# Norms around the first expert stage: sums made with the residual, norm and modulation applied chunk by chunk

## The chip, the cores and the metric

The kernel runs on one NeuronCore of a Trainium2 chip, in float32. The metric is the device time of one execution in microseconds (us). TensorE (PE) multiplies matrices into PSUM, VectorE (DVE) and ScalarE (ACT) work on tiles of 128 partitions, GpSimd (POOL) here mostly issues gathers by index, and SyncE (SP) issues the transfers of weights. The engines run their own instruction lists and meet at semaphores.

## The reference, cut to what matters

The model is two stacks one after the other on 512 tokens of width 1024. What the change touches is the second layer of the first stack from its pooling mixer on, and the start of the second stack:

```
x = layer_norm(DN_ALPHA * x + gt1 * y, ln_g[1, 0], ln_b[1, 0])          # y: the pooling mixer's output
x = layer_norm(DN_ALPHA * x + gt2 * moe_swiglu(x * (1 + sc2) + sh2),    # 8 experts, each token goes to 2
               ln_g[1, 1], ln_b[1, 1])
# second stack
u = _rmsnorm(x, norm1_w)
proj = u @ w_in                                                         # the in-projection
```

`layer_norm` takes mean and variance over the 1024 features of a token, `_rmsnorm` the mean square; x is needed after both, as the residual.

## The kernel before

The residual `k.x` lies with features on the partitions: 8 chunks (KC) of 128 features by 512 tokens. So a mean over features is a sum over partitions, and TensorE makes it: a 128x128 square of ones times each chunk, accumulated over the 8 chunks in one PSUM bank (`k.ps` has 8 banks), which leaves the sum in every partition. A float32 matmul of 128x512 shows as two MATMUL records in the trace, a transpose as one.

The program is a row of stages; nearly each stands in an `nc.Block()` of its own. At a block's end all engines meet before any goes on. Order within a block is the order of the code, engine by engine; there is no scheduler. The stages that matter:

- `stage_pool` (line 1762): modulates x, pools it on VectorE, multiplies by `pl_w` on TensorE, and adds the gated product to x chunk by chunk (L1819).
- `stage_layer_norm(k, 1, 0)` (line 1490): TensorE sums the 8 chunks (L1505); VectorE divides by D (L1517) and subtracts the mean from each chunk (L1520); ScalarE squares (L1533), TensorE sums the squares (L1509), ScalarE takes the root (L1535), VectorE its reciprocal (L1522) and the products (L1525), ScalarE applies g and b (L1539).
- `stage_modulate(k, h, 1, 3)` (line 1547): VectorE makes `h = x * (1 + sc2) + sh2` in 8 instructions (L1553).
- `route(k, r, h)` (line 1932): TensorE multiplies h by the router's weights (L2001, 32 matmuls of 32x128), transposes h into rows (L2008) that ScalarE copies and stores, VectorE picks the experts, ranks them by their counts, and makes the lists of tokens. Once the experts are ranked, SP starts on the first expert's weights.
- the expert block (from line 2772): POOL gathers the rows of the first expert, TensorE transposes them (L2818) and multiplies (L2881 up, L2888 down). VectorE first copies the transposed rows (L3153) and then multiplies x by DN_ALPHA (L2291, `joined.scale_x`). An expert takes 152 tokens at most here; what is beyond goes through a loop at the end. Then `Combine` joins: for each of 4 tiles of 128 tokens POOL gathers the two rows of each token (L2284), VectorE weights and adds them (L2312, L2314), TensorE transposes the sum (L2326), and VectorE adds it to x, gated, chunk by chunk (L2305).
- `stage_layer_norm(k, 1, 1)`, and `stage_rms_norm(k, u, norm1)` (line 3217): ScalarE squares x (L3229), TensorE sums (L3238), root (L3231), reciprocal (L3244), and u is made (L3247). SP issues the first three pieces of `w_in` in this block (L3269).
- the in-projection's block (line 3277): TensorE multiplies u by 6 pieces of `w_in` (L3295), ScalarE copies out.

## Time and profile before

| | us |
|---|---|
| median of 3 runs (lowest, highest) | 3457.12 (3450.19, 3457.69) |
| the profiled execution, its own time | 3453.89 |
| span of the profiled execution | 3452.0 |
| TensorE busy | 2894.8 (84%) |
| VectorE busy | 1115.6 (32%) |
| ScalarE busy | 538.2 (16%) |
| mean granted TensorE clock | 0.911 of full speed |

Times in the trace count from the span's start. The share of busy time is a mean over stages with different limits, so what counts in the rows further down is which engine's instruction ends last before the next stage can start. The granted clock is 1.00 at 2.4 GHz and 0.50 at 1.2 GHz.

### The profile page before, as it was taken

The numbers are of one execution on the slowest core, as the hardware profiler recorded it, in microseconds if no ns is written. First come the engines' busy times: TensorE is split into PE (matmuls) and PEld (weight loads), VectorE is DVE, ScalarE is ACT, GpSimd is POOL, SyncE is SP. The second block draws the span as 40 slices with busy tenths as digits, with TensorE's granted clock in tenths as the row PEclk, the third lists the DMA queues.
The fourth block names the chain that finished last, engine by engine and source line by source line (L and its number), as shares of the span: only waits on it lengthen the run. The fifth ranks groups of instructions, "written<-read, shape, count | busy, mean of one in ns | idle before, by whom it ended". The sixth has DMA issues, their size and how long they took to land. (4 is left out here: it accounts for less than half of the span.)

```text
span 3452.0 us, 58296 instructions
## 1 busy us (share of the span) xinstructions
PE 2894.8 (84%) x25919; PEld 1887.8 (55%) x25919; DVE 1115.6 (32%) x1781; ACT 538.2 (16%) x964; POOL 210.2 (6%) x200
## 2 busy tenths in 40 slices
PE   7998488898887799999579999994897876877784
PEld 2545388888623344445268889882343634544442
DVE  4323578787452001143621111103105623110112
ACT  0001233333121000001100000102003601000001
POOL 0110121111010000000010000000000001000000
PEclk8997699999978899998779999997998987999997
DMA  8622222111221822560099999512301008999994
GB/s 313 196 99 84 82 69 65 48 39 51 73 95 49 204 73 73 178 241 32 28 269 356 345 344 326 216 68 69 117 24 68 1 0 322 427 426 427 427 427 175
DMA packets 241556, 597.92 MB, mean 173 GB/s; under 512 B 24540, under 2 KB 131582, under 8 KB 225816
## 3 DMA queue, kind: packets, MB, share of 16 engines
q1 hardware_dynamic: 210008, 488.85, 38.6%
q0 software_dynamic: 17664, 51.97, 5.3%
q10 hardware_dynamic: 13632, 53.32, 4.0%
q8 instruction: 209, 3.42, 0.4%
q14 instruction: 43, 0.35, 0.0%
HBM read 547.25 MB, written 46.83 MB: 172 GB/s over the span
## 5 line engine op out<-in xcount | busy, mean ns | idle before, releaser
L1658 PE MATMUL ps<-ffn_h,ffn_wb 128*128 128x512 f32 x704 | 306.6, 598 | 33.4 <-DMA ffn_wb<-in_ffn_w 17.9
L2881 PE MATMUL ps<-moe_xt,moe_wb 128*128 128x152 f32 (+2 forms) x2112 | 303.4, 306 | 3.8 <-DMA moe_wb<-in_moe_w 2.1
L2482 PE MATMUL ps<-hier_wb,hier_xt 128*64 128x256 f32 x2048 | 245.1, 396 | 73.1 <-DMA hier_wb<-in_expert_w_up 34.9
L2881 PEld LDWEIGHTS ps<-moe_xt,moe_wb 128*128 128x128 f32 x2112 | 291.5, 192 | 17.0 <-issue 3.9
L2482 PEld LDWEIGHTS ps<-hier_wb,hier_xt 128*64 128x64 f32 x2048 | 162.2, 142 | 167.4 <-issue 70.9
L1658 PEld LDWEIGHTS ps<-ffn_h,ffn_wb 128*128 128x128 f32 x704 | 135.2, 192 | 204.9 <-issue 204.9
L868 PE MATMUL ps<-AT,X 64*64 64x64 f32 x4608 | 164.3, 229 | 34.2 <-DVE X L1160 29.8
L868 PEld LDWEIGHTS ps<-AT,X 64*64 64x64 f32 x4608 | 154.9, 144 | 46.8 <-DVE X L1160 34.6
L1726 PE MATMUL ps<-ffn_g,ffn_wd 128*128 128x512 f32 x352 | 153.0, 598 | 3.0 <-PEq L1617 3.0
L2498 PE MATMUL ps<-hier_wb,hier_actT 128*64 128x512 f32 x512 | 120.3, 613 | 17.9 <-DMA hier_wb<-in_expert_w_down 12.2
L3295 PE MATMUL ps<-in_u,in_wb 128*128 128x512 f32 x256 | 113.1, 604 | 10.0 <-PEq L3222 10.0
L1726 PEld LDWEIGHTS ps<-ffn_g,ffn_wd 128*128 128x128 f32 x352 | 67.4, 192 | 88.6 <-issue 88.6
L2888 PE MATMUL ps<-moe_hT,moe_wb 128*128 128x152 f32 (+1 forms) x880 | 112.8, 290 | 0.0
L2888 PEld LDWEIGHTS ps<-moe_hT,moe_wb 128*128 128x128 f32 x880 | 111.2, 190 | 0.2
L1686 DVE SCALAR_TENSOR_TENSOR ffn_th<-ffn_th,ps 128x512 f32<-128x512 f32 x22 | 15.1, 687 | 293.4 <-ACT ffn_th L1671 293.4
L3161 DVE SCALAR_TENSOR_TENSOR moe_th<-moe_th,ps 128x152 f32<-128x152 f32 (+2 forms) x75 | 25.1, 335 | 249.9 <-ACT moe_th L3039 249.9
L2620 DVE COPY hier_xt<-ps 128x1024 f32<-128x1024 f32 x16 | 19.6, 1225 | 224.9 <-PE ps L2474 224.9
L3295 PEld LDWEIGHTS ps<-in_u,in_wb 128*128 128x128 f32 x256 | 49.6, 194 | 73.3 <-issue 73.3
L1169 DVE TENSOR_TENSOR AT<-AT,ps 128x512 f32<-128x512 f32 x120 | 79.0, 684 | 28.4 <-PE ps L868 26.2
L2498 PEld LDWEIGHTS ps<-hier_wb,hier_actT 128*64 128x64 f32 x512 | 36.4, 139 | 79.0 <-issue 62.8
L1533 ACT ACTIVATE ln_sq<-x 128x512 f32<-128x512 f32 x32 | 19.4, 630 | 381.4 <-DVE x L1520 381.4
L1152 DVE STREAM_TRANSPOSE Y<-AT 128x512 f32<-128x512 f32 x120 | 77.8, 686 | 0.0
(527 smaller groups left out, 4089.7 us busy)
## 6 DMA issues: line engine op xcount, KB each, us to landing
moe_wb<-in_moe_w SPq DMA_DIRECT2D x54, 2048.0 KB, 12.3
hier_wb<-in_expert_w_gate SPq DMA_DIRECT2D x32, 2048.0 KB, 37.8
hier_wb<-in_expert_w_up SPq DMA_DIRECT2D x32, 2048.0 KB, 38.0
hier_wb<-in_expert_w_down SPq DMA_DIRECT2D x32, 2048.0 KB, 38.4
moe_wb<-in_moe_w SPq DMA_DIRECT2D x27, 1536.0 KB, 10.1
ada_late<-in_ada_w ACTq DMA_DIRECT2D x8, 3072.0 KB, 10.2
ffn_wb<-in_ffn_w SPq DMA_DIRECT2D x22, 1024.0 KB, 7.8
ada_rest<-in_ada_w POOLq DMA_DIRECT2D x64, 256.0 KB, 3.3
```

Source lines behind the costliest of these rows:

```text
L868: mm = pe.matmul(k.ps[rows_of(c), g, q * C:(q + 1) * C], X[rows_of(c), at, :], AT[rows_of(c), at, :], start=True, stop=True)
L1152: dve.transpose(group(Y, g), group(AT, g)).then_inc(flipped, 1)
L1169: dve.tensor_tensor(m, m, bank8(g), ALU.add).then_inc(updated, 1)
L1658: mm = pe.matmul(k.ps[:, bank + q, :], wb[:, j, q, c, o * P:(o + 1) * P], h[:, c, :], start=c == 0, stop=c == KC - 1)
L1726: mm = pe.matmul(k.ps[:, j, :], wd[:, j, c, :], g[:, c, :], start=c == 0, stop=c == FC - 1)
L2482: mm = pe.matmul(k.ps[both_halves(a), bank, 0:256], xs[:, c, :], wb[:, slot, at:at + 256], start=c == 0, stop=c == KC - 1)
L2498: mm = pe.matmul(k.ps[both_halves(a), 7, :], at_sb[:, c, :], wb[:, slot, at:at + 512], start=c == 0, stop=c == 3)
L2620: dve.tensor_copy(xt[:, q % 2, :, :].rearrange("p (a c) n -> p a (c n)", a=2), k.ps[:, 4:6, :]).then_inc(xt_ready, 1)
L2881: mm = pe.matmul(k.ps[:, bank, 0:width], wb[:, slot, at:at + P], xs[:, c, 0:width], start=c == 0, stop=c == KC - 1)
L2888: mm = pe.matmul(out_columns(o)[:, 0:width], wb[:, slot, at:at + P], hT[:, f, 0:width], start=f == 0 and o % 3 == 0, stop=f == FC - 1 and ...
L3161: dve.scalar_tensor_tensor(th[:, slot, 0:width], th[:, slot, 0:width], 1.0, k.ps[:, gate, 0:width], ALU.add, ALU.mult)
L3295: mm = pe.matmul(k.ps[:, e % 6, :], own[:, piece] if kind == "fm" else tokens[:, piece], tokens if kind == "fm" else own, start=c == 0, st ...
```

## The change

Four things change.

The pooling stage and `Combine` make the sum over features themselves. In the pooling stage VectorE adds the chunks of x up in a tile of its own after each chunk (`ChunkSums.add`), and TensorE sums that tile over the partitions in one matmul. In `Combine.turn` TensorE runs, for each tile of tokens, 8 matmuls of ones by the finished 128 columns of x into bank 4, one tile behind the transposes.

The block of `stage_layer_norm(k, 1, 0)` and that of `stage_modulate` go. `route` takes a `Norm`: VectorE subtracts the mean straight from PSUM, ScalarE squares, TensorE sums the squares, VectorE multiplies by the reciprocal root, and ScalarE makes h from the scaled x in one instruction per chunk, with g, b, scale and shift folded into two small vectors (`factors`). The router's matmuls wait for h chunk by chunk.

x itself with g and b, times DN_ALPHA, is made by ScalarE at the start of the expert block (`norm.residual`); `joined.scale_x` goes, and `Combine.add` waits for it.

The block of `stage_layer_norm(k, 1, 1)` and that of `stage_rms_norm` go too; both norms run at the head of the in-projection's block, where SP issues the first pieces of `w_in`. ScalarE squares g * x + b in one instruction into u, TensorE sums each chunk as it comes, VectorE meanwhile writes x, and the first in-projection matmul waits for u chunk by chunk.

```diff
@@ stage_pool, vector @@
                     dve.scalar_tensor_tensor(k.x[:, o, :], k.ps[:, o, :], gate[:, o:o + 1], k.x[:, o, :],
                                              ALU.mult, ALU.add)
+                    sums.add(dve, o)
@@ stage_pool, tensor @@
+                sums.total(pe)
@@ new @@
+class Norm:
...
+    def centre(self, dve):
+        k = self.k
+        for c in range(KC):
+            dve.scalar_tensor_tensor(k.x[:, c, :], k.ps[:, self.sums_in, :], -1.0 / D, k.x[:, c, :], ALU.mult, ALU.add).then_inc(
+                k.centred.sem, 1)
+
+    def factors(self, dve, scale=None, shift=None):
+        dve.tensor_scalar(self.own[:, 0, :], self.g, self.alpha, None, ALU.mult)
+        dve.tensor_scalar(self.own[:, 1, :], self.b, self.alpha, None, ALU.mult)
+        if scale is not None:
+            dve.tensor_tensor(self.out[:, 0, :], self.g, scale, ALU.mult)
+            dve.tensor_tensor(self.out[:, 1, :], self.b, scale, ALU.mult)
+            dve.drain()
+            dve.tensor_tensor(self.out[:, 1, :], self.out[:, 1, :], shift, ALU.add)
+        dve.drain()
+
+    def squares(self, act):
+        k = self.k
+        act.activation(self.root[:, :], k.eps[:, 1:2], ACT.Sqrt)
+        for c in range(KC):
+            act.wait_ge(k.centred.sem, k.centred.at(c + 1))
+            act.activation(self.sqr[:, c, :], k.x[:, c, :], ACT.Square).then_inc(k.squared.sem, 1)
+        act.wait_ge(k.square_sums.sem, k.square_sums.at(1))
+        act.activation(self.rstd[:, :], k.ps[:, self.bank, :], ACT.Sqrt, scale=1.0 / D, bias=k.eps[:, 1:2])
+        act.drain().then_inc(k.rooted.sem, 1)
+
+    def sum_squares(self, pe):
+        for c in range(KC):
+            pe.wait_ge(k.squared.sem, k.squared.at(c + 1))
+            mm = pe.matmul(k.ps[:, self.bank, :], k.square("ones"), self.sqr[:, c, :], start=c == 0, stop=c == KC - 1)
...
+    def scale(self, dve, dst=None):
+        dve.wait_ge(k.rooted.sem, k.rooted.at(1))
+        dve.reciprocal(self.rstd[:, :], self.rstd[:, :])
+        dve.drain()
+        for c in range(KC):
+            dve.tensor_tensor(dst[:, c, :], k.x[:, c, :], self.rstd[:, :], ALU.mult).then_inc(k.scaled.sem, 1)
+
+    def modulated(self, act, h):
+        for c in range(KC):
+            act.wait_ge(k.scaled.sem, k.scaled.at(c + 1))
+            act.activation(h[:, c, :], k.x[:, c, :], ACT.Identity, scale=self.out[:, 0, c:c + 1],
+                           bias=self.out[:, 1, c:c + 1]).then_inc(k.h_made.sem, 1)
+
+    def residual(self, act):
+        for c in range(KC):
+            act.wait_ge(k.scaled.sem, k.scaled.at(c + 1))
+            act.activation(k.x[:, c, :], k.x[:, c, :], ACT.Identity, scale=self.own[:, 0, c:c + 1],
+                           bias=self.own[:, 1, c:c + 1]).then_inc(k.x_made.sem, 1)
...
+class ChunkSums:
...
+    def add(self, dve, o):
+        dve.drain()
+        if o == 1:
+            dve.tensor_tensor(self.sums[:, :], k.x[:, 0, :], k.x[:, 1, :], ALU.add)
+        elif o > 1:
+            dve.tensor_tensor(self.sums[:, :], self.sums[:, :], k.x[:, o, :], ALU.add)
+        if o == KC - 1:
+            dve.drain().then_inc(k.summed.sem, 1)
+
+    def total(self, pe):
+        pe.wait_ge(k.summed.sem, k.summed.at(1))
+        pe.matmul(k.ps[:, 0, :], k.square("ones"), self.sums[:, :], start=True, stop=True)
@@ route(k, r, h, norm=None), tensor @@
+                if norm:
+                    norm.sum_squares(pe)
...
+                        if norm and a == 0:
+                            pe.wait_ge(k.h_made.sem, k.h_made.at(c + 1))
@@ route, scalar @@
+                if norm:
+                    norm.squares(act)
+                    norm.modulated(act, h)
@@ route, vector, behind its small set-up instructions; on_vector is centre, factors and scale @@
+                if norm:
+                    norm.on_vector(dve, h)
@@ Combine.turn @@
+        def sums(q):
+            pe.wait_ge(k.free_v.sem, k.free_v.at(q + 1))
+            for c in range(KC):
+                pe.matmul(k.ps[:, sums_in, q * P:(q + 1) * P], k.square("ones"), k.x[:, c, q * P:(q + 1) * P],
+                          start=c == 0, stop=c == KC - 1)
...
             mm.then_inc(k.prod_v.sem, 1)
+            if q and sums_in is not None:
+                sums(q - 1)
+        if sums_in is not None:
+            sums(NT - 1)
@@ stage_first_moe @@
-                stage_layer_norm(k, 1, 0)
-                stage_modulate(k, h, 1, 3)
-                route(k, r, h)
+                norm = Norm(k, "10", k.v("ln_g10"), k.v("ln_b10"), s, alpha=DN_ALPHA, own=own_factors)
+                route(k, r, h, norm)
...
-                    joined.turn(pe)
+                    joined.turn(pe, 4)
...
+                    norm.residual(act)
...
-                    joined.scale_x(dve)
...
+                    dve.wait_ge(k.x_made.sem, k.x_made.at(KC))
                     joined.add(dve)
@@ build @@
-        stage_layer_norm(k, 1, 1)
@@ stage_in_projection @@
-        stage_rms_norm(k, u, k.v("norm1"), load_first)
+        norm = Norm(k, "11", k.v("ln_g11"), k.v("ln_b11"), s, sums_in=4)
@@ its block: sync @@
+                load_first(sp)
@@ tensor @@
+                norm.sum_squares(pe)
+                for c in range(KC):
+                    pe.wait_ge(k.x_made.sem, k.x_made.at(c + 1))
+                    mm = pe.matmul(k.ps[:, 7, :], k.square("ones"), u[:, c, :], start=c == 0, stop=c == KC - 1)
+                mm.then_inc(rms_sums, 1)
...
+                            if e == 0:
+                                pe.wait_ge(scaled_u, c + 1)
@@ scalar @@
+                norm.squares(act)
+                for c in range(KC):
+                    act.wait_ge(k.scaled.sem, k.scaled.at(c + 1))
+                    act.activation(u[:, c, :], norm.sqr[:, c, :], ACT.Square, scale=norm.own[:, 0, c:c + 1],
+                                   bias=norm.own[:, 1, c:c + 1]).then_inc(k.x_made.sem, 1)
+                act.wait_ge(rms_sums, 1)
+                act.activation(rms[:, :], k.ps[:, 7, :], ACT.Sqrt, scale=1.0 / D, bias=k.eps[:, 2:3])
+                act.drain().then_inc(rms_rooted, 1)
@@ vector @@
+                norm.centre(dve)
+                norm.factors(dve)
+                norm.scale(dve, norm.sqr)
+                dve.drain()
+                for c in range(KC):
+                    dve.tensor_scalar(k.x[:, c, :], norm.sqr[:, c, :], norm.own[:, 0, c:c + 1], norm.own[:, 1, c:c + 1],
+                                      ALU.mult, ALU.add)
                 dve.memset(lr[:, :], 1.0)
+                dve.wait_ge(rms_rooted, 1)
+                dve.reciprocal(rms[:, :], rms[:, :])
                 dve.drain()
+                for c in range(KC):
+                    dve.scalar_tensor_tensor(u[:, c, :], k.x[:, c, :], weight[:, c:c + 1], rms[:, :],
+                                             ALU.mult, ALU.mult).then_inc(scaled_u, 1)
```

## Rows read from the trace of the kernel before

**Rows 1.** Page, part 1: engine, busy us (share of the span), instructions.
```profile
PE 2894.8 (84%) x25919; PEld 1887.8 (55%) x25919; DVE 1115.6 (32%) x1781; ACT 538.2 (16%) x964; POOL 210.2 (6%) x200
```

**Rows 2.** Windows: length, busy us of each engine, granted clock, DMA share, GB/s.
```profile
1682.97:1718.76 35.79, 17.87 (x97) 9.19 (x97) 18.04 (x31) 11.28 (x17) 0.00 (x0) 0.81 0.00 1
1760.15:2357.65 597.50, 570.80 (x4208) 509.04 (x4208) 64.21 (x171) 50.33 (x123) 21.00 (x20) 0.98 0.76 269
2383.38:2433.31 49.93, 25.71 (x49) 10.62 (x49) 22.62 (x28) 17.51 (x27) 0.00 (x0) 0.74 0.36 129
```

**Rows 3.** Timeline, VectorE, pool to router: start, us, engine line op tiles xcount [idle before].
```profile
1675.84 4.70 DVE L1819 SCALAR_TENSOR_TENSOR x<-ps,pl_gate,x 128x512 f32<-128x512 f32 x7
...
1691.55 4.91 DVE L1520 TENSOR_TENSOR x<-x,ln_m 128x512 f32<-128x512 f32 x8 [0.44 <-issue]
...
1704.31 4.91 DVE L1525 TENSOR_TENSOR x<-x,ln_r 128x512 f32<-128x512 f32 x8
1711.08 3.74 DVE L1553 TENSOR_SCALAR moe_h<-x,mod 128x512 f32<-128x512 f32 x8 [1.87 <-PEq L1496]
...
1715.57 0.15 DVE L2079 TENSOR_SCALAR moe_iota_b<-iota 8x2 f32<-8x2 f32 x1
```

**Rows 4.** Timeline, TensorE, the same stretch.
```profile
1675.81 6.37 PE L1829 MATMUL ps<-pl_h,pl_w 128*128 128x512 f32 x8 [3.85 <-DVEq L1816]
1683.27 7.10 PE L1505 MATMUL ps<-x,sq 128*128 128x512 f32 x16 [1.09 <-PEq L1778]
1692.96 7.13 PE L1509 MATMUL ps<-ln_sq,sq 128*128 128x512 f32 x16 [2.58 <-ACT ln_sq L1533]
1715.12 3.64 PE L2001 MATMUL ps<-moe_h,moe_wr 128*32 128x128 f32 x64 [15.03 <-PEq L1549]
1718.70 1.11 PE L2008 MATMUL ps<-sq,moe_h 128*128 128x128 f32 x8
```

**Rows 5.** Timeline, ScalarE, the same stretch.
```profile
1705.04 5.75 ACT L1539 ACTIVATE x<-x,vec 128x512 f32<-128x512 f32 x8 [4.22 <-DVE x L1525]
```

**Rows 6.** Windows of 2 us: length, TensorE busy, granted clock, DMA share, GB/s.
```profile
1706.00:1708.00 2.00, 0.00 (x0) 0.50 0.00 0
...
2388.00:2390.00 2.00, 2.00 (x6) 1.00 0.00 0
```

**Rows 7.** Timeline, TensorE, start of the expert stage.
```profile
1760.15 40.08 PE L2881 MATMUL ps<-moe_xt,moe_wb 128*128 128x152 f32 x297 [0.57 <-DVE moe_xt L3153]
```

**Rows 8.** Timeline, VectorE, the same stretch.
```profile
1760.02 2.28 DVE L2291 TENSOR_SCALAR x<-x 128x4096 f32<-128x4096 f32 x1
```

**Rows 9.** Timeline, ScalarE, the same stretch.
```profile
1763.97 0.30 ACT L3039 ACTIVATE moe_th<-ps 128x152 f32<-128x152 f32 x1 [31.31 <-PE ps L2881]
```

**Rows 10.** Timeline, VectorE, joining to in-projection.
```profile
2379.15 4.23 DVE L2305 SCALAR_TENSOR_TENSOR x<-ps,mod,x 128x128 f32<-128x128 f32 x16
...
2393.64 4.90 DVE L1520 TENSOR_TENSOR x<-x,ln_m 128x512 f32<-128x512 f32 x8
...
2406.39 4.90 DVE L1525 TENSOR_TENSOR x<-x,ln_r 128x512 f32<-128x512 f32 x8
2424.02 3.35 DVE L3244 RECIPROCAL rms_r_in_u<-rms_r_in_u 128x512 f32<-128x512 f32 x1 [12.72 <-ACT rms_r_in_u L3231]
2427.45 5.39 DVE L3247 SCALAR_TENSOR_TENSOR in_u<-x,vec,rms_r_in_u 128x512 f32<-128x512 f32 x8
```

**Rows 11.** Timeline, TensorE, the same stretch.
```profile
2374.81 1.97 PE L2326 MATMUL ps<-sq,moe_yg 128*128 128x128 f32 x8 [7.30 <-DVEq L2315]
...
2383.70 9.13 PE L1505 MATMUL ps<-x,sq 128*128 128x512 f32 x16 [2.61 <-PEq L2771]
...
2413.82 9.44 PE L3238 MATMUL ps<-rms_sq_in_u,sq 128*128 128x512 f32 x16 [11.64 <-ACT rms_sq_in_u L3229]
2433.31 6.92 PE L3295 MATMUL ps<-in_u,in_wb 128*128 128x512 f32 x9 [10.05 <-PEq L3222]
```

**Rows 12.** Timeline, ScalarE, the same stretch.
```profile
2399.22 1.28 ACT L1535 ACT_TABLE_LOAD   x1
```

More of the change, by code:

```diff
@@ L198, in build @@
         k.stored = [sem(f"stored{n}") for n in range(2)]
+        k.summed, k.centred, k.squared = dma_sem("summed"), dma_sem("centred"), dma_sem("squared")
+        k.square_sums, k.rooted, k.scaled = dma_sem("square_sums"), dma_sem("rooted"), dma_sem("scaled")
+        k.h_made, k.x_made = dma_sem("h_made"), dma_sem("x_made")
         k.sq = sb("sq", [P, len(SQUARES), P])
@@ L1450, in stage_rwkv_out, with stage_project_residual @@
     k.p_for_v.base += KC
-def stage_project_residual(k, wb, z, gate, alpha=DN_ALPHA):
+def stage_project_residual(k, wb, z, gate, alpha=DN_ALPHA, sums=None):
     with k.nc.Block() as block:
@@ L1471, in _ @@
                 mm.then_inc(k.prod_v.sem, 1)
+            if sums:
+                sums.total(pe)
         @block.vector
@@ new lines, with __init__, close @@
+class ChunkSums:
+    def __init__(self, k, name, stack):
+        self.k, self.sums = k, k.sb(f"x_sums_{name}", [P, SEQ], stack=stack)
+    def add(self, dve, o):
+        k = self.k
+        dve.drain()
[6 more added lines that the diff above has]
+    def total(self, pe):
+        k = self.k
+        pe.wait_ge(k.summed.sem, k.summed.at(1))
+        pe.matmul(k.ps[:, 0, :], k.square("ones"), self.sums[:, :], start=True, stop=True)
+    def close(self):
+        self.k.summed.base += 1
@@ L1777, in stage_pool @@
         stage_modulate(k, h, 1, 0)
+        sums = ChunkSums(k, "pool", s)
         with nc.Block() as block:
@@ L1820, in _ @@
                                              ALU.mult, ALU.add)
+                    sums.add(dve, o)
             @block.tensor
@@ L1831, in _ @@
                         mm.then_inc(k.prod_v.sem, 1)
+                sums.total(pe)
     k.loaded[0].base += 16
@@ L1835, in stage_pool @@
     k.prod_v.base += KC
+    sums.close()
 ROUTER_LOADS = 9
@@ L1929, in overflow_pairs, with route @@
             engine.nop()
-def route(k, r, h):
+def route(k, r, h, norm=None):
     nc, t = k.nc, k.t
@@ L3209, in _ @@
                     overflow_pairs(dve, r, body)
+                    dve.wait_ge(k.x_made.sem, k.x_made.at(KC))
                     joined.add(dve)
             joined.close()
+            norm.close()
 def stage_rms_norm(k, dst, weight, sync=None):
@@ L3274, in load_first @@
             sp.dma_start(wl[:, :, :], src[:, :, att - 2 * GLA_RANK:att]).then_inc(k.loaded[0].sem, 16)
-        stage_rms_norm(k, u, k.v("norm1"), load_first)
+        norm = Norm(k, "11", k.v("ln_g11"), k.v("ln_b11"), s, sums_in=4)
+        rms = k.sb("in_rms", [P, SEQ], stack=s)
+        rms_sums, rms_rooted, scaled_u = (own_signal(k, s, f"in_{n}") for n in ("rms_sums", "rms_rooted", "scaled_u"))
+        weight = k.v("norm1")
         with nc.Block() as block:
@@ L3327, in stage_in_projection @@
     k.prod_v.base += 1
+    norm.close()
 def stage_mixers(k, qk, gg, gv, lr, q_, k_, v, mixed, wb, w):
```

34 lines of the change are left out of this document (32 added, 2 removed).

## The prediction, made before the changed kernel ran

> **What bounds the kernel now.** I read the page's table of engines first: TensorE is busy for 84% of the span [rows 1]. A gain off TensorE counts only where TensorE waits, so I next split the stretch around the change into windows [rows 2]. The expert stage, 597.50 us, is TensorE's: 570.80 busy at clock 0.98. Two stretches are not. From the last addition of the pooling stage to the end of the router's matmuls are 35.79 us, of which TensorE is busy for 17.87. From the last addition of the joining to the first in-projection matmul are 49.93 us, TensorE busy for 25.71, VectorE for 22.62. I call them A and B. In both each engine works while the others wait: one chain, so that each link taken out shortens the kernel until the next link is late. Last I read both stretches engine by engine in order of time; their links are the terms below.
>
> **Stretch A, start.** The seven additions to x start at 1675.84, 0.66 apart (4.70 less one of 0.75, by six), and an eighth ends at 1682.97, the window's start [rows 2, 3]. The change puts a drain behind each, and from the second on an addition. A drain costs 0.08 beyond its instruction (the reciprocal 2424.02 + 3.35, the next start 2427.45) [rows 10]; an addition of 128x512 keeps VectorE 0.60 (4.91 for 8) [rows 3]. So 0.83 for the first chunk and 0.83 + 0.60 for each other: 1675.84 + 0.83 + 7 x 1.43, and 0.16 for the last one's end and drain, is 1686.8, 3.9 later than now. No cover hides this: TensorE's products are done at 1682.18 [rows 4]. Then one matmul of ones, 0.89 at full clock (7.10 by 8) or 1.6 at half (6.37 by 4) [rows 4]; TensorE has stood 4.6 us by then, so I take 1.6: 1688.4. Now the sum ends at 1690.37.
>
> A block's change costs 0.30 (1682.97 to 1683.27), and route's small VectorE instructions, which stand ahead of the norm, end at 1715.72, 0.9 behind the modulation's end at 1714.82 [rows 3, 4]. So the subtraction starts at 1689.3, against 1691.55, since the mean's own instruction is gone as well: 2.2 won. From there to TensorE's first sum of squares are 1.41 now (1691.55 to 1692.96) [rows 3, 4], 1.5 with the sum read from PSUM: 1690.8.
>
> **The clock.** Now these 16 records take 7.13 because TensorE comes from the 7.10 us of the first sum and stands only 2.58 [rows 4]. After the change that work is gone, and what is ahead of the squares is one matmul in 8 us. Where TensorE starts on such work after little activity the same 16 records take 9.13 and 9.44 [rows 11]: half clock for the first 4 us or so, then 1.00 [rows 6]. I take 9.3: 1700.1, as late as now (1700.09). So all that the early sum won is given back by the clock. Beside that, the Trainium skill, "TensorE: Matmul & The Clock Gate", Part 1, says that the engine is at half rate by default and that activity releases it, so that taking work off TensorE can slow the rest. By that rule A's head comes out at nothing won, by the rows at full clock at 2.2; the trace agrees with it as far as 7.13 against 9.13 and 9.44 go.
>
> **Stretch A, end.** From the end of the squares' sum to the scaling 4.22 stay (1704.31 less 1700.09): 1704.3. ScalarE starts 0.73 behind it and takes 5.75 for 8 chunks [rows 3, 5]; now it writes x, then it writes h. The block change, the 3.74 of modulation and the wait of TensorE for all of it go. The router's matmuls, 3.64 by 8 = 0.46 a chunk, follow chunk by chunk: 1704.3 + 0.73 + 5.75 + 0.46 + 0.1 for the handover = 1711.4 in place of 1718.76. The factors, five small instructions of 0.15 to 0.2 with two drains, lie in VectorE's wait for the root (1696.5 to 1700.9). Won: 7.4.
> From this goes what TensorE then lacks in clock. Now the router's 3.64 us at half clock bring it up, and the transposes behind them run at 0.14 each (1.11 for 8) [rows 4]; spread over 5.75 us they may not, and a transpose at half clock takes 0.25 (1.97 for 8) [rows 11]. Eight to sixteen of those stand ahead of what VectorE waits for, at 0.11 each: 0.9 to 1.8. I take 1.0. A gives 6.4; its ends are 3.5 (all of route's short matmuls stay slow) and 9.5 (full clock in both places, 2.2 and 1.0 more).
>
> **The expert stage.** Its weights are requested and its first rows gathered when routing is done, so it moves as a whole. `residual` adds 8 instructions to ScalarE, 5.75 us [rows 5], at the block's start; ScalarE has stood 31.31 us when its first tanh comes [rows 9], which covers them. Without that cover the price would be the 5.75. `scale_x`, 2.28, ends at 1762.30, ahead of the tanh at 1763.97, while TensorE already multiplies [rows 7 to 9]: nothing won by its loss. The joining's new wait on x is met 600 us earlier.
>
> **Stretch B, the sums.** Each tile's 8 matmuls of 128x128 are 16 records. No row shows ones by 128 columns of x; the bounds are the transposes, 0.246 a record at half clock, so 3.9 a tile [rows 11], and the experts' 128x152 at full clock, 40.08 by 297 = 0.135, so 2.2 [rows 7]. Tile 0's lie in TensorE's idle 7.30 [rows 11]. Tile 1's come behind tile 2's transposes, from 2376.8 (2374.81 + 1.97) [rows 11], and at 3.9 end at 2380.7; the last transposes, now free to run when VectorE turns to tile 2's additions at 2379.15 [rows 10], stand behind them, 1.6 late, and end at 2382.7. VectorE's last 8 additions (half of 4.23) then end at 2384.9 and not at 2383.38. By then TensorE has been at it for 6 us, so tiles 2 and 3 go at 2.2: tile 3 from 2384.9 to 2387.1; at half clock throughout it would be 2390.6. I take 2387.5. Now the sum ends at 2392.83 (2383.70 + 9.13).
>
> **Stretch B, the first norm.** With 0.30 of block change the subtraction starts at 2387.8, against 2393.64. But ScalarE now begins this block with a root, and the table for it takes 1.28 [rows 12], now loaded while TensorE sums the squares. With 0.2 for the root itself, ScalarE is free at 2389.4, where the first chunk is ready at 2388.6: 0.8 late. TensorE begins at 2387.8 + 1.5 + 0.8 = 2390.1, warm from the sums, and takes 7.13: 2397.2; cold it would be 2.2 more. Scaling starts at + 4.22 = 2401.4, against 2406.39: 5.0 won.
>
> **Stretch B, the second norm.** Now scaling to in-projection takes 2433.31 - 2406.39 = 26.9: g and b, a block, the squares, the sum, the root, the reciprocal, all 8 chunks of u, a block. Then: ScalarE's first square of g x + b starts 0.73 and ends 1.5 behind the scaling (2402.9); TensorE, cold after 5.7 us of waiting, sums in 9.44 [rows 11]: 2412.4 (warm 7.1; ScalarE alone would end its chunks at 2407.9). Root 0.76 (2423.26 to 2424.02), reciprocal with drain 3.43, first chunk of u 0.75 and handover 0.1 [rows 10]: the in-projection starts at 2417.4. VectorE's eight writes of x, 3.74 as in the modulation [rows 3], lie between the scaling's end at 2406.3 and 2413.1; without that cover they cost 3.74. u comes every 0.67 (5.39 for 8) [rows 10] and TensorE takes 0.77 a record at half clock (6.92 by 9) [rows 11], two to a chunk, so it does not starve. It starts cold now too. The first pieces of w_in come earlier than now and stay hidden. B wins 2433.3 - 2417.4 = 15.9; its ends are 10 (all sums and squares at half clock) and 18.5 (no cold start).
>
> **Sum.** 6.4 + 15.9 = 22.3. Against the profiled execution (3453.89, 1.9 beyond its span) that is 3431.6. The median of the runs shown lies 3.2 above it at 3457.12 and their lowest 3.7 below; the mean of all four is 3454.7. From that: 3432.4, and from the median 3434.8. I say 3433.
>
> **Rivals.**
> 1. TensorE keeps its clock in A's head and in B: 9.5 + 18.5 = 28 won, 3427. For it: it stayed at 1.00 over the 2.58 us pauses [rows 4]. Against: at 1706 it is at 0.50, 6 us after its last matmul [rows 6], and the new pauses are 4.6 and 5.7. Chance 0.12.
> 2. A's gain is taken up by the routing or the first gather (the expert stage waits for something not moved by the router): only B remains, 16 won, 3439. For it: TensorE stands between router and experts. Against: both rows and weights are requested behind the ranks, and the DMA share in A is 0.00 [rows 2]. Chance 0.13.
> 3. Half clock in all that is left of both stretches and no pipelining of the sums: 3.5 + 10 less the late transposes, about 11 won, 3444. Chance 0.06.
> 4. Slower than before: with fewer matmuls ahead of them, the expert stage and the in-projection run their dense matmuls at half clock for long. Place: L2881 and L3295. Price: half of each us of dense work so spent. It decides against the change from 2 x 22.3 = 45 us on; 3465 would need 60. For it: the half clock starts [rows 11]. Against: every dense stretch reaches full clock within about 5 us and the expert stage stands at 0.98 [rows 2]. Chance 0.03.
> That the norms don't overlap as written (an engine barred by an earlier wait) I see no row for: 0.04, 3450. The forecast has the rest, 0.62.
>
> **Numbers.** About 0.2%, 7 us, can be told from no change. Faster by more: forecast, rivals 1 to 3, and most of a quarter of the last, 0.92. Within it: 0.05. Slower: 0.03. The range, 3424 to 3445, holds the forecast's own terms, rivals 1 to 3 and the 7 us between runs.
>
> **What would show it.** Right: A's squares take over 8.5 us on TensorE; the router ends about 29 behind the last pool product where it now ends 36.6; the in-projection starts 38.3 behind the start of tile 2's additions against 54.2 (2379.15 to 2433.31); a table load at the head of B; the expert stage within 1 us of 597.5. Wrong: squares in 7.1, or the stretch between router and experts longer by more than 1.5.

## The result, and the profile after

The changed kernel takes 3421.11 us (median of 4, 3416.30 to 3427.67) against 3455.05 (4 runs of before): ratio 0.9899, interval 0.9884 to 0.9914, 34 us faster. Forecast were 22 us and 3433, range 3424 to 3445: the direction was right, the size too small by 12. Its profiled execution has a span of 3420.7, 31.3 less than before. Of all executions in this document one is left out of its ratio, one of the 12 of before_plus54, which took 4456.19 us at a mean granted clock of 0.634.

Stretch by stretch, in the profiled executions (us; the first addition is the first of L1819, the first weighting that of L2312):

| interval | before | forecast | after |
|---|---|---|---|
| start to the pool's first addition | 1675.8 | same | 1676.8 |
| to the end of the router's matmuls | 42.9 | 35.6 | 35.3 |
| to the experts' first matmul | 41.4 | 42.4 | 40.5 |
| to the joining's first weighting | 597.5 | same | 598.7 |
| to its last weighting | 19.3 | same | 15.8 |
| to the in-projection | 56.4 | 40.5 | 38.2 |
| to the end | 1018.7 | same | 1015.4 |

Stretch A, VectorE, in order of time (start, us, engine line op tiles, count):

```profile
1676.82 1.58 DVE L1935 SCALAR_TENSOR_TENSOR x<-ps,pl_gate,x 128x512 f32<-128x512 f32 x2
1678.47 0.69 DVE L1590 TENSOR_TENSOR x_sums_pool<-x 128x512 f32<-128x512 f32 x1
...
1687.04 0.69 DVE L1592 TENSOR_TENSOR x_sums_pool<-x_sums_pool,x 128x512 f32<-128x512 f32 x1
...
1690.70 4.86 DVE L1512 SCALAR_TENSOR_TENSOR x<-ps,x 128x512 f32<-128x512 f32 x8
...
1704.91 4.90 DVE L1549 TENSOR_TENSOR x<-x,ln_r 128x512 f32<-128x512 f32 x8
```

TensorE in the same stretch:

```profile
1676.79 5.40 PE L1946 MATMUL ps<-pl_h,pl_w 128*128 128x512 f32 x8 [3.85 <-DVEq L1932]
1687.82 2.07 PE L1599 MATMUL ps<-x_sums_pool,sq 128*128 128x512 f32 x2 [5.64 <-DVEq L1594]
1692.18 8.52 PE L1539 MATMUL ps<-ln_sq,sq 128*128 128x512 f32 x16 [2.29 <-ACT ln_sq L1530]
1706.51 5.59 PE L2124 MATMUL ps<-moe_h,moe_wr 128*32 128x128 f32 x64 [5.80 <-ACT moe_h L1555]
1712.03 1.97 PE L2131 MATMUL ps<-sq,moe_h 128*128 128x128 f32 x8
```

Counted from the first addition, the subtraction starts at 13.9 (before 15.7) [rows 3] and the squares' sum ends at 23.9 (before 24.25) [rows 4]: nearly all that was won ahead of the squares is lost in them, at 8.52 against 7.13. The router follows h chunk by chunk and ends 7.2 behind the start of the scaling (1704.91 to 1712.10) where it ended 14.45 behind it (1704.31 to 1718.76) [rows 3, 4]; that is the gain of A. The transposes behind it go at half clock, 1.97 for 8 against 1.11 [rows 4]. That costs nothing further on: the first gather is issued 20.2 behind the router's end in both kernels.

Granted clock around the start of the squares, windows of 2 us (length, busy us of PE, PEld, DVE, ACT, POOL, clock, DMA, GB/s):

```profile
1690.00:1692.00 2.00, 0.00 (x0) 0.00 (x0) 1.66 (x8) 0.79 (x2) 0.00 (x0) 0.50 0.04 7
1692.00:1694.00 2.00, 1.82 (x2) 0.84 (x3) 2.00 (x4) 2.00 (x5) 0.00 (x0) 0.50 0.00 0
1694.00:1696.00 2.00, 2.00 (x5) 0.98 (x4) 1.92 (x8) 2.00 (x4) 0.00 (x0) 0.74 0.00 0
1696.00:1698.00 2.00, 2.00 (x6) 0.80 (x6) 0.11 (x1) 0.23 (x1) 0.00 (x0) 1.00 0.00 0
```

ScalarE makes x in the experts' block, over (1737.14) long before its first tanh (1756.85):

```profile
1731.40 5.74 ACT L1562 ACTIVATE x<-x,moe_ln_own 128x512 f32<-128x512 f32 x8 [6.34 <-PEq L2104]
```

Stretch B with the joining ahead of it, TensorE:

```profile
2353.51 1.97 PE L2461 MATMUL ps<-sq,moe_yg 128*128 128x128 f32 x8 [16.58 <-DVEq L2443]
2356.44 1.97 PE L2461 MATMUL ps<-sq,moe_yg 128*128 128x128 f32 x8 [0.97 <-DVEq L2443]
2358.69 2.97 PE L2454 MATMUL ps<-x,sq 128*128 128x128 f32 x16 [0.28 <-DVE x L2433]
...
2367.27 3.77 PE L2454 MATMUL ps<-x,sq 128*128 128x128 f32 x16 [0.28 <-DVE x L2433]
2370.85 1.06 PE L2461 MATMUL ps<-sq,moe_yg 128*128 128x128 f32 x8
2371.75 1.95 PE L2454 MATMUL ps<-x,sq 128*128 128x128 f32 x16
2374.16 2.05 PE L2454 MATMUL ps<-x,sq 128*128 128x128 f32 x16 [0.47 <-DVE x L2433]
2378.54 7.13 PE L1539 MATMUL ps<-ln_sq,sq 128*128 128x512 f32 x16 [2.33 <-ACT ln_sq L1530]
2391.48 8.75 PE L3435 MATMUL ps<-in_u,sq 128*128 128x512 f32 x16 [5.81 <-ACT in_u L3462]
2405.35 15.07 PE L3447 MATMUL ps<-in_u,in_wb 128*128 128x512 f32 x31 [5.12 <-DVE in_u L3489]
```

The last sum ends 2.1 behind the last addition, the squares run at full clock, and the in-projection starts 31.2 behind the last addition of the joining, against 49.9 [rows 2].

The joining's first transposes show what the forecast didn't look for. The same place before, TensorE and VectorE:

```profile
2363.93 3.58 PE L2326 MATMUL ps<-sq,moe_yg 128*128 128x128 f32 x16 [20.28 <-issue]
```

```profile
2358.49 1.28 DVE L2314 SCALAR_TENSOR_TENSOR moe_yg<-moe_yg,moe_weight 128x1024 f32<-128x1024 f32 x1
```

Before, the first tile is weighted at 2359.8 and TensorE takes it at 2363.93, after 20.28 us idle that nothing in the profile ends ("issue"); after, it takes it at once (2353.51, VectorE's own end is 2353.42). I call this the late start. What stands ahead of it on TensorE is the loop over the experts' overflow, of whose turns one runs (its last matmul ends at 2343.65) and the rest are skipped. The gather for tile 2 waits for these transposes, so the late start carries on to tile 2. GpSimd before and after:

```profile
2366.14 0.94 POOL L2284 DMA_INDIRECT moe_yg<-moe_out,moe_dest  x1 [10.29 <-PE ps L2326]
```

```profile
2355.75 1.42 POOL L2412 DMA_INDIRECT moe_yg<-moe_out,moe_dest  x1 [6.54 <-PE ps L2461]
```

And the queue that brings code (part 3 of the page: packets, MB, share), before and after:

```profile
q8 instruction: 209, 3.42, 0.4%
```

```profile
q8 instruction: 206, 3.38, 0.4%
```

A packet is 3.42 MB by 209 = 16.4 KB. TensorE's compiled list before has 53019 instructions of 64 bytes each, so a packet is 256 of them.

### The profile page after: what moved, and what is told of

Same layout as the page of the kernel before. It is cut to its first block and busy times, and to the rows that moved or that the text cites. A ratio compares the mean times of both kernels' runs of the same rounds, so it can differ in the third digit from the quotient of the medians.

```text
span 3420.7 us, 58348 instructions
## 1 busy us (share of the span) xinstructions
PE 2886.2 (84%) x25953; PEld 1886.2 (55%) x25953; DVE 1117.3 (33%) x1792; ACT 539.0 (16%) x966; POOL 210.4 (6%) x200
## 5 line engine op out<-in xcount | busy, mean ns | idle before, releaser
L1163 DVE TENSOR_TENSOR X<-Y,sq 128x512 f32<-128x512 f32 x120 | 75.1, 665 | 0.0
```

The lines of the kernel that those rows point to most:

```text
L1163: dve.tensor_tensor(group(X, g), m, wide(f"c_off{LEVELS[l]}", 1 - n % 2), ALU.mult).then_inc(masked, 1)
```

## The experiments

Each ratio is to the kernel before on the same chip. Executions of one kernel differ by up to 0.8% here (before: 3443.3 to 3467.3 over all calls), so that a few us show in the traces' intervals and hardly in the medians. The intervals, in us, are from one profiled execution of each kernel (router: first addition to the router's end; experts: from there to the experts' first matmul; late: TensorE's idle ahead of the joining's first transposes; weighting: first to last; norms: last weighting to in-projection). The last column, place, is where the last branch of the loop over the experts' overflow stands in TensorE's compiled list:

```
kernel            router   experts   late   weighting  norms   q8 packets  place
before             42.9     41.4     20.3     19.3      56.4     209       42276
after              35.3     40.5     16.6     15.8      38.2     206       42239
a_only             36.5     40.8     16.6     16.0      56.0     206       42239
b_only             41.9     41.4     22.4     20.7      42.1     209       42276
join_sums_late     35.5     40.4     16.5     16.1      45.2     206       42239
pool_sums_late     33.5     43.1     22.4     19.5      42.0     209       42266
after_pad28        35.4     40.4     16.5     15.7      38.2     206       42239
before_pad228      42.0     42.3     23.2     22.0      56.4     209       42276
kept_warm          35.7     40.9     23.0     22.1      38.5     209       42303
pool_pe_chunks     31.7     42.8     22.1     20.7      41.9     209       42267
after_plus1        36.6     40.2     16.7     15.5      38.5     206       42243
before_plus54      43.1     43.0     17.5     16.2      58.6     207       42492
fed_root_late      36.6     40.7     16.5     16.0      37.8     207       42239
joined_best        33.6     43.5     16.6     15.9      37.7     208       42495
```

Where the late column shows 16.5 to 17.5, VectorE's weighting ended the wait; where it shows 20 and more, nothing that the profile names.

**a_only**: stretch A's part alone.

```diff
-                    joined.turn(pe, 4)
+                    joined.turn(pe)
...
+        stage_layer_norm(k, 1, 1)       # and the in-projection's stage of before
```

> The change's part around the first norm alone (pool sums, norm and modulation inside routing, x made by ScalarE in the expert block, scale_x gone); the joining, the norm behind it, the RMS norm and the in-projection are those of the kernel before. Theory 1 (the gain is the sum of two stretches, and the 11 us beyond the forecast lie in the second one and around the joining): 7.6 up to the router's end and 0.9 behind it, 8.5 us faster than before, ratio 0.9975. TensorE's start on the joining's first transposes stays as late as before (4.1 us behind VectorE's weighted sum), if that wait belongs to the joining's code before. Theory 2 (that late start is scatter between executions): it is gone or of another size here, with no link to the time. Theory 3 (half of the excess lies in the first stretch): 13 or more.

Measured: 3443.63 us (12 runs), ratio 0.9971 (0.9960 to 0.9982), 10 us. Its own terms are 6.4 to the router's end and 0.6 behind it; and the late start is gone, 3.2, though not a line of the joining is changed. Theory 1 holds for the first stretch (forecast 8.5), and was wrong in tying the late start to the joining's code. The squares take 9.80 here, more than in the changed kernel.

**b_only**: stretch B's part alone.

```diff
-                norm = Norm(k, "10", ...)
-                route(k, r, h, norm)
+                stage_layer_norm(k, 1, 0)
+                stage_modulate(k, h, 1, 3)
+                route(k, r, h)
...                                      # no sums in the pool, no residual; scale_x is back
```

> The change's part behind the expert stage alone (sums in the joining, both norms at the head of the in-projection's block); pool, first norm, modulation and scale_x as before. Theory 1: 18.2 us from the start of tile 2's additions to the in-projection, and 4 more if the late start of TensorE in the joining goes: 22 us faster, ratio 0.9936; without that 18, 0.9948. Theory 3: 14 to 16. The two parts' gains should add up to that of the whole (34) within 4.

Measured: 3437.01 (8 runs), 0.9951 (0.9933 to 0.9969), 17 us. The norms' interval falls by 14.3, not 18. The late start stays. What is missing there against the changed kernel is 3.8, of which 3.0 is TensorE's clock, seen in its rows: squares 8.83 for 7.13, RMS sums 10.06 for 8.75.

```profile
2363.43 3.65 PE L2457 MATMUL ps<-sq,moe_yg 128*128 128x128 f32 x16 [22.38 <-issue]
...
2388.87 8.83 PE L1539 MATMUL ps<-ln_sq,sq 128*128 128x512 f32 x16 [2.32 <-ACT ln_sq L1530]
2403.51 10.06 PE L3429 MATMUL ps<-in_u,sq 128*128 128x512 f32 x16 [5.80 <-ACT in_u L3456]
2418.68 3.75 PE L3441 MATMUL ps<-in_u,in_wb 128*128 128x512 f32 x4 [5.11 <-DVE in_u L3483]
```

The two parts give 10 and 17, the whole 34. Against the changed kernel b_only lacks 4.9 in the weighting and 3.8 in the norms, while 3.2 of the weighting are in a_only's 10: 27 + 4.9 + 3.8 - 3.2 = 32.5, which is the whole within its interval.

**join_sums_late**: the changed kernel, the sum behind the joining made at the head of the next block.

```diff
-                    joined.turn(pe, 4)
+                    joined.turn(pe)
@@ in-projection's block, tensor @@
+                for c in range(KC):
+                    mm = pe.matmul(k.ps[:, 4, :], k.square("ones"), k.x[:, c, :], start=c == 0, stop=c == KC - 1)
+                mm.then_inc(k.summed.sem, 1)
```

> The changed kernel, but the sum over features behind the joining is made by 8 matmuls of 128x512 at the head of the in-projection's block, as the layer norm did before, and not tile by tile in the joining. Theory 1: the sums in the joining end 6.9 us behind the start of tile 2's additions, the sum of before ended 13.7 behind it; so this is 6 to 7 us slower than the changed kernel (about 27 faster than before, ratio 0.992). Rival (the matmuls in the joining delay its transposes and cost what they save): within 2 us of the changed kernel. If TensorE's start in the joining is late again here, that costs 3 to 4 more and ties the wait to how many instructions TensorE has behind the loop.

Measured: 3425.07 (6 runs), 0.9917 (0.9900 to 0.9935). Norms 45.2 against 38.2, so the tile-wise sums are worth 7.0, as said; 0.7 of it is the RMS sums' clock (9.48 for 8.75). The ratios differ by 6 us the same way, but their intervals overlap.

**pool_sums_late**: the changed kernel, the sum ahead of the first norm made at the head of routing.

```diff
-                    sums.add(dve, o)
-                sums.total(pe)
+                    for c in range(KC):
+                        mm = pe.matmul(k.ps[:, 0, :], k.square("ones"), k.x[:, c, :], start=c == 0, stop=c == KC - 1)
+                    mm.then_inc(k.summed.sem, 1)
                     norm.sum_squares(pe)
```

> The changed kernel, but the sum ahead of the first norm is made by 8 matmuls at the head of routing, and the pooling stage adds no chunks on VectorE. Theory 1 (what the early sum wins, TensorE's clock takes back): the subtraction starts 0.8 later, the squares go at full clock in 7.1 and not 8.5 us: 0.6 us faster than the changed kernel, so no difference that can be measured. Rival (the early sum is worth the 2.2 us that it wins): 1.5 to 2.5 us slower than the changed kernel.

Measured: 3424.97 (6 runs), 0.9913 (0.9893 to 0.9932), by which it can't be told from the changed kernel. To the router's end 33.5, 1.8 less than in the changed kernel. TensorE's rows:

```profile
1665.80 5.40 PE L1944 MATMUL ps<-pl_h,pl_w 128*128 128x512 f32 x8 [4.13 <-DVEq L1931]
1672.29 7.11 PE L2115 MATMUL ps<-x,sq 128*128 128x512 f32 x16 [1.09 <-PEq L1893]
1680.84 7.13 PE L1539 MATMUL ps<-ln_sq,sq 128*128 128x512 f32 x16 [1.45 <-ACT ln_sq L1530]
```

The subtraction starts 13.6 behind the first addition, even ahead of the changed kernel's 13.9, and the squares go at 7.13. So up to the router's end the pool's sums on VectorE are a loss of 1.8, and the rest of the change carries A. At the experts' first matmul nothing of it is left: that comes 76.7 behind the first addition, against 75.8. The first gather is issued as far behind the router's end in both (20.4 and 20.2), and what TensorE then waits for are its rows. The changed kernel, then this one:

```profile
1747.74 1.02 PE L2957 MATMUL ps<-sq,moe_xg 76*128 76x76 f32 x6 [19.10 <-DMA moe_xg<-moe_rows,moe_slot_token]
```

```profile
1737.66 1.02 PE L2957 MATMUL ps<-sq,moe_xg 76*128 76x76 f32 x6 [21.53 <-DMA moe_xg<-moe_rows,moe_slot_token]
```

All three kernels with the pool's sums on TensorE and the new norm have 42.8 to 43.5 from the router's end to the experts, the others with the new norm 40.2 to 40.9. Why the rows land later there was not tested; before_plus54, with the norm of before, has 43.0 too.

And the late start is back, with 7 matmuls more ahead of the expert block. So far it is there in three of three kernels with 209 packets and in none of three with 206, which speaks against mere scatter.

**after_pad28 and before_pad228**: empty instructions to move TensorE's code.

```diff
+                if norm:
+                    for _ in range(28):
+                        pe.nop()
```

> The changed kernel with 28 empty instructions in TensorE's list at the end of routing, where it then waits 19 us for the first rows; they move all of its later code back by as many places and cost nothing by themselves. Theory 1 (TensorE's late start on the joining comes from where its code lies: on leaving the loop over the experts' overflow it has to fetch code, in three packets more or less): like the kernel whose pool sums are late, TensorE stands 20 us or more ahead of the joining's first transposes, 209 instruction packets in place of 206, and 3 to 4 us slower than the changed kernel. Theory 2 (scatter between executions, or the work of the norms itself): 16.5 us and 206 packets as in the changed kernel, no difference.

> The kernel before with 228 empty instructions in TensorE's list, 114 at the head of the pooling stage and 114 at the end of routing, both in waits of over 13 us. Theory 1, if code is fetched in packets of 16 KB, which would be 256 places of 64 bytes: 228 forward is 28 back, the late start is gone (16.5 us of idle, bounded by VectorE), 206 or 207 packets, and 3 to 4 us faster than before with no change to the work. Theory 2: late start as in the kernel before, no gain.

Measured: 3418.15 (4 runs), 0.9897 (0.9877 to 0.9917), and 3458.36 (10 runs), 1.0013 (1.0000 to 1.0026). Nothing can be read from them on the question: the empty instructions are not in the compiled lists, which are the same as those of the changed kernel and of the one before (53065 and 53019 instructions on TensorE). They are the two kernels once more, and so show what a comparison is worth: 0.13% from nothing. They also show that the late start comes again with the same list, but not in the same size: TensorE starts 6.4 behind VectorE's weighted tile in before_pad228, 4.2 before.

**kept_warm**: dead matmuls in three of TensorE's waits.

```diff
+                    for _ in range(16):     # ahead of the router; bank 0, 16 ahead of the RMS sums; 14 ahead of the in-projection
+                        pe.matmul(k.ps[:, 2, 0:P], k.square("ones"), k.square("ones"), start=True, stop=True)
```

> The changed kernel with matmuls that nobody reads (128x128, into free banks) while TensorE waits for a root: 16 ahead of the router, 16 ahead of the RMS sums, 14 ahead of the in-projection. Theory 1 (in what is left of both stretches the clock decides): router's transposes at full clock win 0.5 to 1, the RMS sums take 7.1 and not 8.75 to 10 us, the in-projection starts at full clock and wins 1.7: 4 us faster than the changed kernel (3417), ratio to before 0.989 or less. Rival (the squares come too slowly for the clock to matter, ScalarE bounds the sums): under 1 us.

Measured: 3425.33 (6 runs), 0.9920 (0.9903 to 0.9937). No gain: the 16 ahead of the router bring nothing there (35.7), and the late start is back (23.0). In B it has 38.5, where the three other kernels with the new norms and a late start have 41.9 to 42.1. That is not all the feeding: its squares take 7.13 ahead of any dead matmul of that block, and its RMS sums 8.83, no less than unfed (8.75). Only the in-projection gained a clock: it ran at 1.00 from its start at 2406.1, where the changed kernel's, started at 2405.35, stood at 0.50 until 2408.

**pool_pe_chunks**: TensorE sums the pooled x inside the pooling stage.

```diff
-                    sums.add(dve, o)
-                sums.total(pe)
+                for o in range(KC):
+                    pe.wait_ge(k.summed.sem, k.summed.at(o + 1))
+                    pe.matmul(k.ps[:, 0, :], k.square("ones"), k.x[:, o, :], start=o == 0, stop=o == KC - 1)
```

> The changed kernel, with TensorE and not VectorE summing the pooled x, 8 matmuls chunk by chunk inside the pooling stage, each behind its addition; VectorE's additions and drains go. Theory 1: the additions end 3.9 us earlier, TensorE, warm by then, ends its 8 matmuls about 7.1 us behind the last product of the pool (1682.2 to 1689.5 on the changed kernel's scale, where it now ends at 1689.9), and the squares follow at full clock: 7.1 in place of 8.5. 1.5 to 2 us faster than the changed kernel; it has 7 matmuls more ahead of the loop, so the late start of TensorE in the joining comes back and takes 3 to 4: together 1 to 2 us slower. Rival: if the late start is not tied to the code's place, 1.5 to 2 us faster.

Measured: 3429.46 (6 runs), 0.9919 (0.9893 to 0.9945). Router's end at 31.7, 3.6 earlier (1.7 of it is the pool's own products at 3.70 for 5.40, by the clock they met), and the late start, 22.1. Of the 3.6, 2.3 is lost again up to the experts' first matmul (42.8 for 40.5); the weighting takes 4.9 more and the norms 3.7 more. So it is no gain in the end, as theory 1 had it, and by more than theory 1 said.

**after_plus1 and before_plus54**: TensorE's code moved by real instructions, each of them a dead matmul of two columns inside a wait of 13 us or more.

```diff
+                    for _ in range(1):      # before_plus54: 27 here and 27 at the head of the pooling stage
+                        pe.matmul(k.ps[:, 5, 0:2], k.square("ones"), k.square("ones")[:, 0:2], start=True, stop=True)
                     for n in range(3):
                         x_rounds(0, n)
```

> The changed kernel with one dead matmul (ones by two columns, into a free bank) on TensorE at the head of the expert block, where it waits 19 us for rows. It moves TensorE's later code by 4 places of 64 bytes. In the compiled list the last branch of the loop over the overflow is then at place 42243; in the three kernels without a late start it is at 42239, one short of 165 x 256, in those with one at 42266 to 42303 (16.4 KB, a packet of the instruction queue, is 256 places). Theory 1 (the place of the loop's end against the packets' edges makes the late start): idle ahead of the joining's first transposes 20 us or more, 209 packets, and with the half clock behind it some 3 to 7 us slower than the changed kernel, for work of 0.4 us inside a wait. Theory 2 (the work ahead, such as 8 matmuls for the pooled sums, makes it): 16.5 us, 206 packets, no difference.

> The kernel before with 54 dead matmuls of two columns, 27 at the head of the pooling stage (TensorE waits 13.8 us there) and 27 at the head of the expert block (19.9 us): 216 places, which puts the loop's last branch at 42492, short of 166 x 256 = 42496. Theory 1: the late start goes (16.5 us of idle in place of 20.2, 207 packets or fewer) and the kernel before gets 3 to 4 us faster by added work; ratio 0.9989. Theory 2: late as before, no gain or a loss.

Measured: after_plus1 3420.59 (6 runs), 0.9907 (0.9892 to 0.9922), no late start: theory 1 missed. Four places are not enough, 27 are (pool_sums_late, at 42266 and not 42239). before_plus54 3449.27 (12 runs), 0.9980 (0.9967 to 0.9992): the kernel before, with work added and nothing taken away, is 7 us faster by the ratio. The late start explains 3.1 of that in its profile (weighting 16.2 for 19.3), and the wait is now VectorE's:

```profile
2357.26 1.97 PE L2328 MATMUL ps<-sq,moe_yg 128*128 128x128 f32 x8 [17.46 <-DVEq L2317]
```

So the late start follows where TensorE's code lies and not how much work it has: dead matmuls, with which it came in kept_warm, here make it go. In all 14 profiled executions the place of the loop's end tells the two kinds apart: 42266 to 42303 late, 42239 to 42243 and 42492 to 42495 in time, with 165 x 256 = 42240 and 166 x 256 = 42496. The Trainium skill, "Advanced Engine Details and Errata", section ISA Cache, says that TensorE's instruction cache holds 128 KB in lines of 16 KB, 256 instructions. The trace agrees with the line by the packets' 16.4 KB; the loop over the overflow is some 2350 instructions long, over nine such lines, more than that page gives the cache. That the time goes into fetching code is argued from this and from the packets, and not shown: no transfer of a packet was tied to the wait. Which of the edges decides was not found; no run here shows the cache's size.

**fed_root_late**: the changed kernel, without the early root, fed only behind the loop.

```diff
-                norm.squares(act)
+                norm.squares(act, False)    # False: no root of eps ahead of the squares
+                for _ in range(16):         # and 14 ahead of the in-projection
+                    pe.matmul(k.ps[:, 0, 0:P], k.square("ones"), k.square("ones"), start=True, stop=True)
```

> The changed kernel without the early root in the second norm, and with dead matmuls while TensorE waits in the in-projection's block (16 ahead of the RMS sums, 14 ahead of the first piece); nothing ahead of the loop is moved. Theory 1: the squares start 0.8 us earlier (the table is loaded behind them), the RMS sums take 7.1 to 7.4 and not 8.75, the in-projection's first 4 us run at full clock: 2 to 4 us faster than the changed kernel. Rival: the root in its old place makes ScalarE load the table after the squares where TensorE already waits for nothing, and the sums are bound by ScalarE: under 1 us.

Measured: 3417.43 (4 runs), 0.9890 (0.9873 to 0.9906). Norms 37.8 against 38.2, so the rival is nearer. The squares start 0.6 earlier (2.02 to 1.41 behind the subtraction), as said of the table. The feeding did not do what it should. TensorE's rows, and its windows of 2 us (length, TensorE busy, granted clock, DMA, GB/s):

```profile
2383.49 3.73 PE L3435 MATMUL ps<-sq 128*128 128x128 f32 x32
2389.46 8.83 PE L3438 MATMUL ps<-in_u,sq 128*128 128x512 f32 x16 [2.24 <-ACT in_u L3467]
```

```profile
2390.00:2392.00 2.00, 2.00 (x4) 0.51 1.05 389
2392.00:2394.00 2.00, 2.00 (x4) 0.64 0.94 263
```

The dead matmuls go at 0.117 a record and not 0.135, are over at 2387.2, and the clock falls at 2390, with the real sums already running since 2389.46. Ahead of the in-projection it went the same way: started at 2403.41, it stood at 0.50 from 2404 to 2407.

**joined_best**: fed_root_late with the sums of pool_pe_chunks, and 57 dead matmuls ahead of the loop.

```diff
+                for _ in range(28):         # head of the pooling stage; 29 at the head of the expert block
+                    pe.matmul(k.ps[:, 1, 0:2], k.square("ones"), k.square("ones")[:, 0:2], start=True, stop=True)
```

> The last one, and the pooled sums made by TensorE chunk by chunk; 57 dead matmuls (28 at the head of the pooling stage, 29 at the head of the expert block) put the loop's last branch at 42495, short of 166 x 256. Theory 1: the 3.6 us that the pooled sums on TensorE win up to the router's end (31.7 against 35.3) are kept and the late start stays away: 4 to 7 us faster than the changed kernel, 3415. Theory 2: late start as in pool_pe_chunks (22 us), no better than the changed kernel.

Measured: 3411.89 (6 runs), 0.9880 (0.9858 to 0.9901). The late start stays away (16.6) with the loop's end placed as forecast. The router's end is at 33.6 and not the 31.7 of pool_pe_chunks, whose products of the pool met full clock (3.70, here 5.64). It beats both kernels, the changed one by 7 us by the ratios and 9 by the medians. Its profile (span 3409.0 against 3420.7) bears out less: 1.7 to the router's end and 0.5 in the norms, 3.0 lost again from the router's end to the experts. The rest lies elsewhere: 8.0 ahead of the pool's first addition, where the two have the same code but for dead matmuls in a wait, 2.1 in the expert stage and 2.4 behind the in-projection's start. Over the 14 kernels the first addition comes anywhere from 1665.8 to 1676.8. The intervals of the two ratios overlap, so its lead over the changed kernel is not shown; that over the kernel before is.

## Why the prediction fell short

The direction, the places of the gain and most sizes were right. The time missed the range by 3 us.

- Stretch A, start: right. VectorE's sums end 10.9 behind the first addition (1687.04 + 0.69 less 1676.82), forecast 11.0; one matmul of 2.07 for 1.6 (the 6.37 that this was worked out from had met full clock from 1681 on); squares cold at 8.52 for 9.3. Rival 1, full clock in A, did not come. pool_sums_late shows more than was forecast: up to the router's end the early sum not only wins nothing, it costs 1.8, though not up to the experts.
- Stretch A, end: right, 35.3 for 35.6. The 1.0 charged to the transposes did not appear: they ran at half clock, 1.97 for 8, but the first gather was issued 20.2 behind the router's end as before, so the term is 0.0. The interval to the experts came out 0.9 shorter and not 1.0 longer since the gather's rows landed that much sooner; over all the kernels it runs from 40.2 to 43.5.
- The expert stage and `scale_x`: nothing that shows (598.7 for 597.5, 0.2 beyond the 1 us allowed; over the kernels it runs from 596.6 to 600.8).
- Stretch B, the sums: end 6.9 behind the start of tile 2's additions, forecast 8.4. The pass of tile 1 took 3.77 (forecast 3.9), and delayed tile 3's additions by 0.4 only, since the transposes behind it ran at full clock (1.06 for 1.97). So the 1.6 was mis-sized.
- Stretch B, the norms: the early root's table did hold the squares back, by 0.6 (forecast 0.8); RMS sums 8.75 for 9.44. Together 38.2 for 40.5, and 36.0 from the start of tile 2's additions, for 38.3. b_only at 42.1 lies on the forecast's other side: the same code takes 38.2 to 42.1, mostly by the clock it meets, so that 38.2 is in part luck.
- The step that failed is one I did not take: the prediction puts any change from the joining's first weighting up to tile 2's additions at nothing, without a reason. I read the window from tile 2's additions backwards only to the transposes that I needed, and took the interval before as given, although one row there had TensorE idle for 20.28 with no releaser. That was 4.1 us of waiting behind a tile that was ready, and the change removed it without meaning to, by making TensorE's list 37 places shorter ahead of the loop's end (42276 to 42239). 3.4 us in the weighting came from it directly; without them the median would be about 3424.5, an estimate, at the range's low end. That these came the right way is luck. Three kernels that start late and have the new norms also spend 41.9 to 42.1 in B against 38.2 to 38.5. That this too follows from the late start is not shown: kept_warm is late and has squares of 7.13 and 38.5 in all, before_plus54 is in time and has squares of 8.83.
- Rival 4 did not come: the in-projection was at 1.00 from 2409 on, 3.7 us behind its start. Its "within about 5 us" was read too low, since the kernel before took 5.7 there (2433.31 to 2439).
- Of the missing 9 us of the profiles 3.4 are this, 2.3 is B's norms, and 1.9 the interval from the router's end to the experts. 3.3 lie behind the in-projection's start, 2.3 of them in the in-projection and what follows up to the first softmax (216.0 to 213.7); kernels with the new head have 213.5 to 215.4 there, before_plus54 with the old one 214.8, and this part was not taken apart. 0.3 more came up to the router's end, and 2.2 went the other way, ahead of A and in the expert stage. The medians' difference, 34, is 3 beyond the profiles' 31, which is less than either kernel's spread.
- The range was too narrow for its own terms: its low end of 3424 came from rivals worked out singly against a kernel whose executions spread over 20 us.

## What to carry to other kernels

Where a chain of short stages waits on every engine in turn, pipelining chunk by chunk and dropping block changes pays what the rows say: 7 and 14 to 18 us here. Taking matmuls off TensorE ahead of such a chain pays nothing if the next sums then run at half clock (8.52 for 7.13): ask what it did just before. Read a gain at the point where the next long stage starts, and not only at the end of the stretch: 1.8 us won up to the router were gone at the experts. And look up every idle time of the engine that nothing in the profile ends, above all behind loops whose turns are skipped: here it followed where the code lies, and edits ahead of it moved the time by 3 to 6 us, either way.

## What the runs showed of the hardware beyond that

- Behind a loop of some 2350 TensorE instructions, of whose turns one ran and the rest were skipped, TensorE came 4 to 7 us late to ready work in six runs (209 instruction packets in all of them), and in time in eight (206 to 208). 27 to 64 places more than the changed kernel's brought it; 216 more than before took it away.
- Dead matmuls in a wait did not reliably hold TensorE's clock for the work behind it. Ahead of the RMS sums they failed in three runs of three (8.83, unfed 8.75): in fed_root_late the sums started 2.2 us behind them at 1.00 and were at 0.51 within 1 us, though running. Ahead of the in-projection they failed in two, and in kept_warm the clock stayed at 1.00.
- Empty instructions of TensorE leave no place in the compiled list (53065 instructions with and without 28 of them).
